# Mixture-of-experts stage: alternate blocks filled from the last slot down, eighteen half pieces of weights in flight, second blocks at the eleventh and nineteenth place

## The reference

```python
def hierarchical_moe(h, w_group, b_group, w_route, b_route, w_gate, w_up, w_down):
    # h: (512, 2048); 32 experts in 4 groups; each token goes to 2 experts of one group
    expert_id = g_idx[:, None] * EXPERTS_PER_GROUP + top_idx      # (512, 2)
    ...
    def expert_block(args):
        xb, e = args                                             # xb: rows of h sent to e
        act = jax.nn.silu(xb @ w_gate[e]) * (xb @ w_up[e])       # w_gate, w_up: (2048, 256)
        return act @ w_down[e]                                   # w_down: (256, 2048)
    ...
    return jnp.einsum('nkd,nk->nd', picked, weights)
# and then, in second_block:
#   x = x + gate2 * m
```

## Time and profile before

| what | us |
|---|---|
| median of three runs (lowest, highest) | 2162.5 (2162.3, 2162.56) |
| the profiled execution | 2158.96 |
| its span, first to last instruction | 2157.2 |
| PE busy | 1986.6 (92%) |
| DVE busy | 817.4 (38%) |
| ACT busy | 313.7 (15%) |
| POOL busy | 174.1 (8%) |

### The profile page before, as it was taken

One profiled execution on the slowest core, in us unless ns is written; L12 is line 12 of the kernel. 1 busy time (PEld: TensorE's weight loads), 2 busy tenths in 40 slices (PEclk: granted clock), 3 DMA queues, 4 the chain that ended last, 5 costly groups with the idle time before them and its releaser, 6 DMA issues.

```text
span 2157.2 us, 19478 instructions
## 1 busy us (share of the span) xinstructions
PE 1986.6 (92%) x7654; PEld 1019.2 (47%) x7654; DVE 817.4 (38%) x1377; ACT 313.7 (15%) x604; POOL 174.1 (8%) x190
## 2 busy tenths in 40 slices
PE   6999999999999999999999999999959987777885
PEld 3444545544444455444444445554435544444553
DVE  0375737442377355446251002522253332222222
ACT  0011111130210232100150112321210000000000
POOL 0000022000000000000000000000002211111111
PEclk9999999999999999999999999999979999999898
DMA  6575645334115443957122221143189999999994
GB/s 238 187 276 203 239 143 186 103 119 174 59 59 201 158 148 109 359 213 290 52 78 79 77 79 59 39 157 131 74 316 383 363 408 406 400 403 391 395 391 164
DMA packets 116407, 448.07 MB, mean 208 GB/s; under 512 B 20918, under 2 KB 21276, under 8 KB 77020
## 3 DMA queue, kind: packets, MB, share of 16 engines
q1 hardware_dynamic: 86460, 303.80, 36.9%
q0 software_dynamic: 24288, 118.32, 15.9%
q10 hardware_dynamic: 5568, 24.69, 3.0%
HBM read 440.39 MB, written 26.28 MB: 216 GB/s over the span
## 4 chain that ended last, share of the span: by engine, by line
PE 77%; SPq 17%; DMA 2%; issue 1%; ACT 1%; DVE 1%; ACTq 0%; POOL 0%; POOLq 0%; DVEq 0%
PE bank L974 40%; SPq L598 16%; PE bank L977 15%; PE bank L1005 6%; PE bank L1173 4%; PE bank L796 3%; PE bank L1184 2%; DMA RW<-in_w_up 1%; PE bank L842 1%; PE bank L869 1%; PE bank L1087 1%; PE bank L829 1%; DMA RH<-in_x 1%; PE bank L811 1%; PE bank L1167 0%
## 5 line engine op out<-in xcount | busy, mean ns | idle before, releaser
L974 PE MATMUL bank<-RW,RX 128*128 128x512 f32 (+1 forms) x1536 | 631.0, 567 | 5.5 <-ACT RA L1243 3.0
L974 PEld LDWEIGHTS bank<-RW,RX 128*128 128x128 f32 x1536 | 278.5, 190 | 328.7 <-issue 327.2
L977 PE MATMUL bank<-RX,RW 128*128 128x512 f32 x768 | 338.7, 594 | 1.6 <-ACT RA L1243 1.3
L1671 DVE SCALAR_TENSOR_TENSOR RG<-RG,ccol 128x2048 f32<-128x2048 f32 x90 | 212.4, 2360 | 125.2 <-DMA RG<-in_w_mod 119.8
L974 PE MATMUL bank<-RW,RM 128*128 128x512 f32 x576 | 249.9, 593 | 1.5 <-PE bank L974 1.2
L977 PEld LDWEIGHTS bank<-RX,RW 128*128 128x128 f32 x768 | 143.9, 191 | 169.1 <-issue 167.5
L974 PEld LDWEIGHTS bank<-RW,RM 128*128 128x128 f32 x576 | 108.4, 190 | 137.9 <-issue 137.1
L2384 DVE TENSOR_TENSOR RA<-RA,bank 128x128 f32<-128x128 f32 x34 | 9.8, 287 | 331.7 <-ACT RA L1633 331.6
L1243 ACT ACTIVATE RA<-bank 128x512 f32<-128x512 f32 (+3 forms) x167 | 83.1, 537 | 297.6 <-PE bank L796 82.4
L716 POOL DMA_DIRECT2D RG<-in_w_mod x96 | 51.5, 536 | 883.9 <-DVE RG L1671 534.2
L1173 PE MATMUL bank<-RW,RG 128*64 128x256 f32 x640 | 79.5, 406 | 22.2 <-DMA RW<-in_w_up 22.1
(11 more groups left out here) (258 smaller groups left out, 1625.0 us busy)
## 6 DMA issues: line engine op xcount, KB each, us to landing
RG<-in_w_mod POOLq DMA_DIRECT2D x96, 1024.0 KB, 5.3
RW<-in_w_in SPq DMA_DIRECT2D x72, 1024.0 KB, 5.0
RW<-in_w_out SPq DMA_DIRECT2D x24, 1024.0 KB, 5.2
RX<-in_w_gate SPq DMA_DIRECT2D x19, 1024.0 KB, 29.2
RX<-in_w_up SPq DMA_DIRECT2D x19, 1024.0 KB, 28.6
RW<-in_w_gate SPq DMA_DIRECT2D x19, 1024.0 KB, 29.0
RW<-in_w_up SPq DMA_DIRECT2D x19, 1024.0 KB, 28.3
RM<-in_w_down SPq DMA_DIRECT2D x18, 1024.0 KB, 30.4
```

Source lines behind the costliest of these rows:

```text
L974: ins = nc.tensor.matmul(banks[j][:, 0:width], act[:, ka, j * P:(j + 1) * P], W[:, s, kt % 4, 0:width], start=kt == 0, stop=kt == kk - 1)
L977: ins = nc.tensor.matmul(banks[j][:, :], W[:, s, kt % 4, j * P:(j + 1) * P], act[:, kt, :], start=kt == 0, stop=kt == kk - 1)
L1671: st.do(v.scalar_tensor_tensor(out=dst, in0=x, scalar=sc, in1=y, op0=op0, op1=op1), s, n)
```

## The change

Three things are changed at once.

1. **Slots.** In every second column from column 3 on (`KEPT:NCOL:2`), the rows fill the slots from 63 downward. For that, a second matrix OSB holds the slots counted from the end; `slots` runs its eight matmuls once more with it, and DVE takes the columns concerned from this second result. In the other columns, and in the first three blocks, the slots are filled from 0 upward as before.
2. **Pieces.** PIECES is 18. The four new ones lie in RH, where the residual stood; SP issues pieces 14 to 17 after all four stores of `out` have landed (`out_stored`).
3. **Order.** The experts with a second block stand at the places 10 and 18 (counted from 0), no longer at 3 and 4.

```diff
+TWIN_AT = (10, 18)
-PIECES = 14
+PIECES = 18
+        "spot_back": np.broadcast_to((BLK - 1.0 - np.arange(BLK)).astype(np.float32)[None, :], (P, BLK)),
...
-        homes = [RX[:, 0:4096], RX[:, 4096:8192], RG[:, 0:4096], RW[:, 0:4096], RW[:, 4096:8192], RM[:, 0:4096], RM[:, 4096:8192]]
+        homes = [RX[:, 0:4096], RX[:, 4096:8192], RG[:, 0:4096], RW[:, 0:4096], RW[:, 4096:8192], RM[:, 0:4096], RM[:, 4096:8192], RH[:, 0:4096], RH[:, 4096:8192]]
...
-        slot_w = spent[1][:, 0:NCOL]
+        found = RA[:, 7456:7456 + 2 * NCOL].rearrange("p (v b) -> p v b", v=2)
+        slot_w = found[:, 1]
+        OSB = RA[:, 0:1024].rearrange("p (m s) -> p m s", m=8)
...
+        STREAM = [e for e in range(NE) if not KEPT <= e < KEPT + TWINS]
+        for k in range(TWINS):
+            STREAM.insert(TWIN_AT[k], KEPT + k)
         BLOCKS = []
-        for pos in range(NE):
-            BLOCKS.append((pos, pos))
-            if KEPT <= pos < KEPT + TWINS:
-                BLOCKS.append((pos, NE + pos - KEPT))
+        for pos, col in enumerate(STREAM):
+            BLOCKS.append((pos, col))
+            if KEPT <= col < KEPT + TWINS:
+                BLOCKS.append((pos, NE + col - KEPT))
...
             expert_piece(12)
             expert_piece(13)
+            sp.wait_ge(sem("out_stored"), 16 * TT)
+            for n in range(14, 18):
+                expert_piece(n)
             for n in range(PIECES, 6 * NE):
...
-                    expert_at[0] = sp.value_load(permi[n // 6:n // 6 + 1, 0:1], min_val=0, max_val=NE - 1)
+                    col = STREAM[n // 6]
+                    expert_at[0] = sp.value_load(permi[col:col + 1, 0:1], min_val=0, max_val=NE - 1)
...
-                for m in range(8):
-                    ins = nc.tensor.matmul(bk[:, 0:2 * NCOL], OS[:, m, :], BVW[:, m].rearrange("p v b -> p (v b)"), start=m == 0, stop=m == 7)
+                for back, spots in ((0, OS), (2 * NCOL, OSB)):
+                    for m in range(8):
+                        ins = nc.tensor.matmul(bk[:, back:back + 2 * NCOL], spots[:, m, :], BVW[:, m].rearrange("p v b -> p (v b)"),
+                                               start=m == 0, stop=m == 7, skip_group_check=True)
...
-            tt_(eq, eq, per(wab[:, :], [P, 8, NCOL]), ALU.mult, sem("onehots_ready"))
+            tt_(eq, eq, per(wab[:, :], [P, 8, NCOL]), ALU.mult)
+            tt_(spots_back, slot[:, :].unsqueeze(2).unsqueeze(2).to_broadcast([P, 8, 2, BLK]), spot_back, ALU.is_equal)
+            st.settle()
+            dve.sem_inc(sem("onehots_ready"), 1)
...
-            st.do(v.tensor_copy(slot_w, bk[:, NCOL:2 * NCOL]))
-            index_columns(bk[:, KEPT:NCOL], "slots", KEPT, NCOL)
+            both = bk[:, 0:4 * NCOL].rearrange("p (o v b) -> p o v b", o=2, v=2)
+            st.do(v.tensor_copy(found, both[:, 0]))
+            st.settle()
+            st.do(v.tensor_copy(found[:, :, KEPT:NCOL:2], both[:, 1, :, KEPT:NCOL:2]))
+            st.settle()
+            index_columns(found[:, 0, KEPT:NCOL], "slots", KEPT, NCOL)
```

More of the change, by code:

```diff
@@ L547, in column @@
             return BLOCKS[n][1] if n < NST else n
-        OVER_PIECES = ((10, 11, 12, 13, 0, 1), (2, 3, 4, 5, 6, 7))
+        OVER_PIECES = ((12, 13, 14, 15, 16, 17), (0, 1, 2, 3, 4, 5))
+        piece_landed = [sem(f"piece{s}") for s in range(14)] + w_landed
+        landed_dense = [0] * 14 + landed
         in_static = [len(range(s, 6 * NE, PIECES)) for s in range(PIECES)]
@@ L597, in expert_piece @@
                 e = pos if pos < KEPT else expert_at[0]
-                sp.dma_start(pieces[n % PIECES], halves[which][e]).then_inc(sem(f"piece{n % PIECES}"), 16)
+                sp.dma_start(pieces[n % PIECES], halves[which][e]).then_inc(piece_landed[n % PIECES], 16)
             n = 0
@@ L673, in _ @@
                         sp.wait_ge(sem("half_up"), i * 2 + (NST - 1 + u))
-                        sp.dma_start(pieces[at[GATE0]], wgv[0][e]).then_inc(sem(f"piece{at[GATE0]}"), 16)
-                        sp.dma_start(pieces[at[UP0]], wuv[0][e]).then_inc(sem(f"piece{at[UP0]}"), 16)
+                        sp.dma_start(pieces[at[GATE0]], wgv[0][e]).then_inc(piece_landed[at[GATE0]], 16)
+                        sp.dma_start(pieces[at[UP0]], wuv[0][e]).then_inc(piece_landed[at[UP0]], 16)
                         sp.wait_ge(sem("up_done"), i * 2 + (NST - 1 + u))
-                        sp.dma_start(pieces[at[GATE1]], wgv[1][e]).then_inc(sem(f"piece{at[GATE1]}"), 16)
-                        sp.dma_start(pieces[at[UP1]], wuv[1][e]).then_inc(sem(f"piece{at[UP1]}"), 16)
+                        sp.dma_start(pieces[at[GATE1]], wgv[1][e]).then_inc(piece_landed[at[GATE1]], 16)
+                        sp.dma_start(pieces[at[UP1]], wuv[1][e]).then_inc(piece_landed[at[UP1]], 16)
                         sp.wait_ge(sem("down_done"), i * 2 + (NST - 1 + u))
-                        sp.dma_start(pieces[at[DOWN0]], wdv[0][e]).then_inc(sem(f"piece{at[DOWN0]}"), 16)
-                        sp.dma_start(pieces[at[DOWN1]], wdv[1][e]).then_inc(sem(f"piece{at[DOWN1]}"), 16)
+                        sp.dma_start(pieces[at[DOWN0]], wdv[0][e]).then_inc(piece_landed[at[DOWN0]], 16)
+                        sp.dma_start(pieces[at[DOWN1]], wdv[1][e]).then_inc(piece_landed[at[DOWN1]], 16)
         @block.gpsimd
@@ L1188, in landed @@
             def landed(n):
-                pe.wait_ge(sem(f"piece{n % PIECES}"), 16 * (n // PIECES + 1))
+                pe.wait_ge(piece_landed[n % PIECES], landed_dense[n % PIECES] + 16 * (n // PIECES + 1))
             turn(0, 16, None)
@@ L1224, in _ @@
                             for n in (at[2 * h], at[2 * h + 1]):
-                                pe.wait_ge(sem(f"piece{n}"), i * 16 + 16 * (in_static[n] + 1))
+                                pe.wait_ge(piece_landed[n], i * 16 + (landed_dense[n] + 16 * (in_static[n] + 1)))
                             gate_up(u, h, half_in(at[2 * h]), half_in(at[2 * h + 1]))
@@ L2362, in _ @@
             tt_(spots, slot[:, :].unsqueeze(2).unsqueeze(2).to_broadcast([P, 8, 2, BLK]), spot_no, ALU.is_equal)
+            spots_back = OSB.rearrange("p m (h s) -> p m h s", h=2)
+            spot_back = C["spot_back"].unsqueeze(1).unsqueeze(1).to_broadcast([P, 8, 2, BLK])
             st.settle()
```

## The result

| what | before | after |
|---|---|---|
| median, us (runs) | 2162.4 (2160.46 to 2162.56, 4) | 2133.78 (2131.98 to 2134.71, 4) |
| ratio, 95% interval | | 0.9869 (0.9852 to 0.9886) |
| span of the profiled execution, us | 2157.2 | 2132.6 |

The account below looks back on a forecast made before the run. Weight transfers in the mixture-of-experts stage were taken as the bound. Terms -8.9 + 1.0 - 25.7 = -33.6 us, taken as -34, gave 2125 for the profiled execution and 2128.5 for the median, range 2120 to 2143.

Parts of the forecast that it names:

- What bounds the kernel: Mixture-of-experts stage: weight transfers bound it, not PE; what counts is when the last weights land.
- The three idle places: DMA engines do nothing ahead of block 0, at 1681 to 1686 us, and at the end of the weights.
- Pieces 14 to 17: Ahead of block 0: four pieces issued at about 1597.5 fill the hole; 9.8 less 0.9 for piece 18, gain 8.9 us.
- the hole at 1681: At 1681 to 1686 us engines run empty while PE works at second blocks, which free no pieces.
- Sixteen matmuls: On PE in block 0, before its hidden values: 1.98 us more; cost at the end 0 to 2.3, taken as 1.0.
- Slots and order: Whole weight stage, priced together by volume: 198.8 MB at 402 GB/s, 494.5 us instead of 520.2, gain 25.7 us.
- a fall from full to nothing in some 5 us: Sign at the weights' end: engines stop nearly together, last weights at about 2105 in place of 2139.5.
- The 17.7 us behind the weights: After the last weights: last down products, scaling and last addition, 17.7 us, claimed to stay.
- The price of a row: Engine time per 4 KB packet, two packets a row: 0.32 us at most, 0.15 at the plain rate.
- The slots don't matter: Rival: the tail stays; only the gains ahead of block 0 and at 1681 come: 2151.5 us, chance 0.08.
- Slower: Rival: the two last engines are slow themselves and get more rows from the new filling: 2179.5 us, chance 0.03.
- A new stall: Rival: second blocks at 10 and 18, or seams between experts, stall transfers 5 to 7 us each: 2140, chance 0.05.

Follow-up runs that it names:

- the order alone: Changed kernel with 14 pieces and all slots filled from 0 up, extra matmuls kept; only the second blocks' new places left: 2159.12 us, 0.9989 of before.
- the pieces alone: Changed kernel with second blocks back at places 3 and 4 and all slots filled from 0 up, extra matmuls kept: 2153.89 us, 0.9964 of before.
- The interleaved version: Changed kernel with other slot tables: row r goes to engine group r modulo 8, every second column counted from the other end: 2128.0 us, 0.9852 of before.
- the repeat: The changed kernel, unaltered, run once more beside other versions on the same chip: 2133.55 us, 0.9868 of before.
- three matmuls: Changed kernel with three matmuls of 512 columns into an unused bank ahead of the last block: 2132.47 us, 0.9868 of before.
- all but the slots: Changed kernel with all blocks filled from slot 0 up, keeping 18 pieces and the new order: 2148.25 us, 0.9936 of before.
- the mirrored filling: 14 pieces, old order, all blocks but the first three filled from slot 63 down, none from 0: 2163.59 us, 1.0013 of before.
- The slots alone: Changed kernel with 14 pieces and second blocks back at places 3 and 4; only the filling from both ends left: 2148.55 us, 0.9938 of before.

## Why the prediction was right, and where it was off

**What bounds the kernel**: right. The three idle places were there, and closing them is what gained. After the change, the long stretch has 402 GB/s.

**Pieces 14 to 17**: right in mechanism and close in size. The stores landed at 1599.1, in an execution 1.1 us later, so at 1598.0 on the forecast's clock; 1597.5 was forecast, and the earlier trace rows allow 1596.6 to 1598.0. The pieces filled the hole, piece 18 went out 1.1 us later than piece 14 had, offset taken away. Alone this part made 7.6 us where 8.9 was the term (7.9 with the sixteen matmuls counted); the hole at 1681, deeper by 1.7 us, fits what is missing.

**Sixteen matmuls**: right about what they take, and too dear in the sum. 3.76 us in place of 1.98, and block 0's down products 2.2 us later once the offset is taken off (1618.31 against 1615.05):

```profile
1604.07 8.52 PE bank L1188 x64
1612.60 3.76 PE bank L1172 x32
```

The transfers did not notice (share 0.97 behind it), so the 1.0 us that I took was too much for the changed kernel. With 14 pieces, in the order alone, some 3 us went there (0.5 of them because that execution stood later), which is the upper bound of 2.3 or a little over.

**Slots and order, priced by volume**: the rate of 402 GB/s came out exactly. The term of 25.7 us was too large all the same: less the 7.6 us of the pieces alone, 21.0 of the 28.6 us are left for it. What failed is the step from a rate to an end: "a fall from full to nothing in some 5 us", with the last weights at about 2105. The fall took 12 us and the weights ended at 2112, 5.5 us late when the 1.1 us are taken off (2139.5 less 34 is 2105.5). I had checked evenness by sums over the whole stage (123 to 136 rows an engine), but the end depends on the last blocks, each of which loads at most half of the engines (by the partition rule, two to four of the eight of a half). The interleaved version, with the same rate (403 GB/s) and the same matmuls, falls in 6 us and ends the weights at 2106, some 3.7 us sooner once block 0's start is taken off. That is the part of the 5.5 us which is shown to come from the last blocks; the other 1.8 stay open.

**The 17.7 us behind the weights "stay"**: wrong by 2.9 us in this execution (20.6), by 1.6 in the repeat (2114.2 to 2133.5) and by 0.9 with the interleaved table. They were measured in a kernel where PE had finished gate and up before the last pieces landed. With even engines the last block's pieces come close together, and PE's own 12.3 us from the second piece on (6.93 + 1.7 + 3.65) stand behind them, part of it at half clock after a wait of 3.63 us. In the repeat, with a wait of 3.67 us, the last gate and up took 8.81 us and not 10.07. With PE kept busy by three matmuls 19.1 us stood behind the weights, no clear gain on the repeat's 19.3, so how much of the 2.9 us is the clock is not settled. The spans give the sum: 2157.2 - 2132.6 = 24.6 us, and 2139.5 - 2112 = 27.5 us at the weights' end, less 2.9 behind it, are the same. The medians differ by 28.6, 4 us more; the spread of the profiled executions about their medians is of that size, and I leave it there.

**The price of a row.** The forecast kept 0.15 to 0.32 us a packet open; 0.47 us a row of two packets is 0.24 a packet, measured where one pair of engines is the bound, and it is a mean of two that differ: 0.16 for a packet gathered, 0.33 for one added.

**Rivals.** *The slots don't matter* would have given 2151.5; it gave 2133.8, and all but the slots 2148.25. *Slower* fell: the changed kernel is faster, and the mirrored filling cost 2.5 us, not over 10. *A new stall* didn't come: no stretch that I read between 1612 and 2100 is under 0.9. That the changes would work on each other I had priced only as one volume. That the total came within 5.4 us is in part luck. The slots alone, priced at 15 to 20 us in their own expectation, made 12.9, and in the profiled executions the sum is 8.4 us short (5.5 in the fall, 2.9 behind the weights); the medians, in which before stands 3.4 us above its profiled execution and after 0.6 below, take some of that back.

## What to carry to other kernels

Where transfers bound a stage, look at how the DMA engines end, not only at how busy they are: here a share that fell in steps of two sixteenths over 20 us was the sign that the load hung on which partitions carried rows. Gathers with fewer rows than slots are then worth dealing over the partitions, even within each block; here a table of constants did it, with no second table and no extra matmuls (2130.68 us). And a gain in one place can be spent in another: measure a ring's depth, the order of blocks that free nothing, and the balance together as well as alone.

## What the runs showed that I had not expected

- A row added costs its DMA engine twice what a row gathered does: 0.33 against 0.16 us for 4 KB.
- A float32 matmul stands in the trace as two records (seven are x14, eight of `slots` x16), so a duration "of one" is half of it: one of 512 columns and 128 partitions of output takes 0.9 us at the full clock (6.28 us for seven), where I had reckoned with 0.45. The eight of the down products, each of which fills 64 partitions, take 3.65 us together, 0.46 each; why they are faster no run here tests.
- A part that is right by itself (four more pieces) made another hole deeper, from 3.2 to 4.9 us without work, and the part worth 2.4 us alone (the order) is the one that closed it.
- The granted clock fell to 0.50 ahead of the last block, with PE idle for 3.63 us. It was not the only fall: in the changed kernel there are eight more between 1620 and 2100, for 3.4 or 6.8 us each, the first, the second and the fourth at waits of 4.21, 2.67 and 3.13 us or within 1.1 us behind them; the mean there is 0.96. With three matmuls in the last wait and 0.60 us of it left, it stayed up.
